# Two-layer retention and attention trunk: slice loads between weight blocks, a reordered first norm, and repeated identity products on TensorE

## The chip, the cores and the metric

The kernel runs on one core of one Trainium2 chip. The metric is the device time of one execution in microseconds. Before the change three runs gave 1913.54, 1915.96 and 1918.54 us, so the median is 1915.96 us.

## The reference, cut to what matters

Two layers (DEPTH = 2), d_model 1024, on 384 tokens in all: one prompt of 256 tokens and eight sample sequences of 16 tokens. All is float32.

```python
for l in range(DEPTH):
    mods = silu(c) @ w_ada[l] + b_ada[l]            # 1024 -> 6*1024, one row per sequence (9 rows)
    sh1, sc1, gt1, sh2, sc2, gt2 = split(mods, 6)
    h  = rmsnorm(x, g_mix) * (1 + sc1) + sh1
    u  = h @ w_in          # ret q,k,v,gate | att q,k,v | two merge gates
    y_r = gate * groupnorm(retention(rotary(q_r), rotary(k_r), v_r))      # 8 heads
    y_a = attention(rmsnorm(q_a), rmsnorm(k_a), v_a, rel_bias)            # 8 heads, own band / cache
    mixed = sigmoid(m_r) * (y_r @ w_br_ret) + sigmoid(m_a) * (y_a @ w_br_att)
    x  = x + gt1 * (mixed @ w_out)
    h2 = rmsnorm(x, g_ffn) * (1 + sc2) + sh2
    x  = x + gt2 * (relu(h2 @ w_up)**2 @ w_down)
```

The outputs are the final x of both groups, the retention states and the key and value rows.

## The kernel before, in words

**Split products.** Each float32 weight block and each activation is held as a high part (rounded to fp32r) and a low part (the rest). A product is three matmuls: high x high, low x high, high x low. SyncE (SP) loads weight blocks of 512 KB into a ring of four `raw` slots (`load`, L395 to L400; L395 waits until the block four places earlier has been split). ScalarE copies a block to `whi` (`high`, L679), VectorE subtracts to get `wlo` (`low`, L956); both have two slots. TensorE uses a block in `token_products` (L1407, 18 matmuls that stream 512 columns) or `products` (L1383, 24 matmuls that stream 384 columns).

**Order of the work.** It is written out by hand, one instruction stream for each engine, tied by semaphores. For each layer: the norm; the stage S_V (attention values, 8 blocks); 8 heads (8 blocks each, the attention and retention of the head before woven between the blocks); S_MERGE (2 turns of 20 blocks); S_OUT (`w_out`, 2 turns of 4 blocks); the second norm; S_UP (8 turns of 4 blocks); S_DOWN (4 turns of 8 blocks).

**The modulation.** `w_ada` is cut in slices of 512 columns, 2 MB each. A slice is multiplied by silu(c) on TensorE (`ada_product`, L1430), VectorE copies the result to `ada_s` (`ada_rows`, L1004), TensorE transposes it (`ada_turned`), VectorE adds the bias and writes `modT` (`ada_cols`, L1010). Layer 0's first four slices are loaded whole before the first norm needs them (two halves: slices 0 and 2, then 1 and 3). The last two slices of each layer go into `adaf_w`, which lies over memory that the merge still reads; so SP waits for `m_ready` (the last `mlo` of the merge) and issues the four 1 MB transfers (L467) in S_OUT, behind the fourth block of turn 0 and ahead of the first block of turn 1. Their products (`last_modulation`) come behind the second norm's sums.

**The first norm.** Squares of x are summed on ScalarE, POOL raises the mean to the power -1/2 (`x_rs`), VectorE puts it on a diagonal (`x_diag`), TensorE spreads it over the partitions with a ones matrix (L1517, into bank X[0]), VectorE copies it to `rstd` (L991). POOL writes the relative-position bias to DRAM (`band_d`), waits for that, and issues the copy to `skew_d` ahead of its part of the norm. TensorE waits for `rstd` before the first two slices of the modulation, since they use bank X[0]. When `modA` is there (L1020), VectorE splits blocks 0 and 1 and then makes the tiles k = 0 to 3 of the normed activation: `hp` (L1030) for the prompt; POOL makes `hs` (L542 multiply, L546 add) for the samples; ScalarE makes `hhi`; VectorE makes `hlo` (L1035, L1036) and so releases `h_ready`, for which the products wait.

**The head's start.** S_V uses six banks, the last two being X[1] and X[2]. ScalarE copies them out as `va_tok`. TensorE waits for the copies of banks 4 and 5 ahead of the first block of head 0, in both layers, though the head first uses X[0] and X[1] behind its sixth block.

Of the kernel before, what the change touches and what calls it, by code (L numbers as in the profile page):

```python
# [13 lines left out]
P = 128  # L14
# [134 lines left out]
def trunk(nc, x_prompt, x_sample, state_ret, cache_attn_k, cache_attn_v, c_prompt, c_sample, w_ada,  # L149
# [236 lines left out]
    def _(sp):  # L386
# [32 lines left out]
        for l in range(DEPTH):  # L419
# [38 lines left out]
            for i in range(S_OUT.turns):  # L458
                with cnt.turn(S_OUT.adds) as c:
                    for j in range(4):  # L460
                        load(c, j, [rows(w_out, l, j % 2, i * (2 * BC) + j // 2 * BC)])
                        if i == 0 and j == 3:
                            sp.wait_ge(m_ready, M0 + (l + 1) * KT)
                            for f in range(ADA_F):
                                at = (ADA0 + ADA_M + f) * ADA_C
                                for k in range(2):
                                    sp.dma_start(adaf_w[:, f, k * 4:k * 4 + 4, :],  # L467
                                                 w_ada[l, k * 4 * P:(k + 1) * 4 * P, at:at + ADA_C]
                                                 .rearrange("(k p) n -> p k n", p=P)).then_inc(adaf_full[f], 16)
            with sp.Fori(0, S_UP.turns) as i, cnt.turn(S_UP.adds) as c:  # L470
                for j in range(4):
                    load(c, j, [rows(w_up, l, j % 2, i * (2 * BC) + j // 2 * BC)])
# [20 lines left out]
    def _(pool):  # L493
# [30 lines left out]
        def first_tables(c):  # L524

            pool.wait_ge(band_ready, 1)
            dma(band_d, band[:, :]).then_inc(band_out, 16)
            pool.wait_ge(xms_ready, 1)
            g.tensor_tensor(x_rs[:, 0:NT], x_ms[:, 0:NT], mhalf[:, 0:NT], ALU.pow).then_inc(xrs_ready, 1)
            pool.wait_ge(band_out, 16)  # L530
            dma(skew_d, bass.AP(tensor=band_d.tensor, offset=CHUNK - 1, ap=[[BAND, DEPTH * HEADS], [-1, CHUNK], [1, SKEW]]))\
                .then_inc(skew_out, 16)
            pool.wait_ge(rstd_ready, 2)
            for k in range(KT):
                c.op(g.tensor_tensor(hs[:, k, :], xT[:, k, PR:TOK], rstd[:, PR:TOK], ALU.mult))
            for half in range(2):
                pool.wait_ge(moda_ready, half + 1)
                c.settle()
                for k in range(half * 4, half * 4 + 5):
                    d = seqs(hs[:, k % KT, :])  # L540
                    if k < half * 4 + 4:
                        c.op(g.tensor_tensor(d, d, modA[:, k, 1:NSEQ].unsqueeze(2).to_broadcast([P, SB, ST]), ALU.mult))  # L542
                    if k > half * 4:
                        pool.wait_ge(pool_own, c.now["own"] + (c.mine - 1 if k < half * 4 + 4 else c.mine))
                        d = seqs(hs[:, k - 1, :])
                        g.tensor_tensor(d, d, modT[:, k - 1, 1:NSEQ].unsqueeze(2).to_broadcast([P, SB, ST]),  # L546
                                        ALU.add).then_inc(hs_ready, 1)

        def norm_sample(c, shift):

# [392 lines left out]
    def _(dve):  # L943
# [44 lines left out]
                        x_rs[:, 0:NT].unsqueeze(2).to_broadcast([P, NT, P]), ALU.mult).then_inc(diag_ready, 1)  # L988
        dve.wait_ge(pre_a, 3)
        dve.wait_ge(spread_done, 1)  # L990
        v.tensor_copy(rstd[:, :], X[0][:, 0:TOK]).then_inc(rstd_ready, 2)  # L991

        def ada_rows(l, s, x):

# [44 lines left out]
        def norm(c, shift, gain, first=False):  # L1039

            if first:
                for half in range(2):
                    for n, s in enumerate(ADA_ORDER[2 * half:2 * half + 2]):
                        ada_rows(0, s, X[3 - 3 * n])
                        ada_cols(0, s, X[3 - 3 * n])
                    dve.wait_ge(mod_ready, 2 * half + 2)
                    modulated(c, shift, gain, half * 4, half * 4 + 4).then_inc(moda_ready, 1)
                    if half == 0:
                        low(c, 0)
                        low(c, 1)  # L1050
                    else:
                        low(c, 4)
                    dve.wait_ge(rstd_ready, 2)
                    dve.wait_ge(moda_ready, half + 1)
                    normed_tiles(c, shift, half * 4, half * 4 + 4)
                    if half == 0:
                        low(c, 2)
                        low(c, 3)
                return
            modulated(c, shift, gain, 0, KT).then_inc(moda_ready, 2)  # L1060
            low(c, 1)
            inverse_std(c)
            dve.wait_ge(rstd_ready, c.norm * 2 + 2)
            dve.wait_ge(moda_ready, c.norm * 2 + 2)
            if shift == 0:
                normed_tiles(c, shift, 0, 4)
                low(c, 2)
                low(c, 3)
                normed_tiles(c, shift, 4, KT)
            else:  # L1070
                normed_tiles(c, shift, 0, KT)
# [262 lines left out]
    def _(pe):  # L1334
# [181 lines left out]
        def mm(out, lhsT, rhs, start=True, stop=True):  # L1516
            return t.matmul(out, lhsT, rhs, start=start, stop=stop, skip_group_check=True)  # L1517

        def head(c, h, prev):

            H = c.head
            gr = S_HEAD.groups
# [18 lines left out]
                last_states(c)  # L1541
            gemm(5)

            pe.wait_ge(qk_norm, H + 1)
            pe.wait_ge(pair_ev, H * 4 + (P0 - 2))
            for n in range(NT):
# [60 lines left out]
        def last_modulation(l):  # L1607

            for f in range(ADA_F):
                pe.wait_ge(adaf_full[f], l * 32 + 32)  # L1610
                for k in range(KT):
                    ins = ada_product(X[1 + f], k, adaf_w[:, f, k, :], k == 0, k == KT - 1)
                ins.then_inc(ada_mm, 1)

        def up(c, l, first):
            for j in range(4):
# [16 lines left out]
                    ada_turned(l + 1, i, X[3])  # L1633


        pe.wait_ge(diag_ready, 1)
        for n in range(NT):
            ins = mm(X[0][:, n * P:(n + 1) * P], ones[:, :], x_diag[:, n, :])
        ins.then_inc(spread_done, 1)
        with cnt.turn({"norm": 1}, use=("norm",)) as c:  # L1640
            pass
# [1 line left out]
        def first_modulation(half):  # L1643

            if half == 0:
                pe.wait_ge(rstd_ready, 2)
            else:
                pe.wait_ge(mod_ready, 2)
            slices = ADA_ORDER[2 * half:2 * half + 2]
            for n, s in enumerate(slices):  # L1650
                for k in range(KT):
                    if k % 4 == 0:
                        pe.wait_ge(ada0_full[s][k // 4], 16)
                    ins = ada_product(X[3 - 3 * n], k, ada0_w[:, s, k, :], k == 0, k == KT - 1)
                ins.then_inc(ada_mm, 1)
            for n, s in enumerate(slices):
                ada_turned(0, s, X[3 - 3 * n])

        for l in range(DEPTH):
            if l:  # L1660
                with cnt.turn({"norm": 1}, use=("norm", "head")) as c:
                    norm(c)
            with cnt.turn(S_V.adds, also=("norm",)) as c:
                for j in range(8):
                    if l == 0 and j in (0, 3):
                        first_modulation(j // 3)
                    token_products(c, j, S_V.groups[j % 2], j // 2, normed=j % 2 == 0 and j < 6)
            with cnt.turn(S_HEAD.adds) as c:
                pe.wait_ge(acc_free[4], l + 1)
                pe.wait_ge(acc_free[5], l + 1)  # L1670
                head(c, 0, None)
            with pe.Fori(0, HEADS - 1) as h, cnt.turn(S_HEAD.adds) as c:
                head(c, h + 1, h)
            for i in range(S_MERGE.turns):
# [54 lines left out]
```

## Time and profile before

| what | value |
|---|---|
| median of 3 runs | 1915.96 us |
| the profiled execution's own time | 1917.57 us |
| its span | 1915.9 us |
| mean granted TensorE clock | 0.986 |
| TensorE busy | 1831.2 us, 96% |
| VectorE, ScalarE, POOL busy | 980.7, 735.0, 359.2 us |

The profiled execution's time is 1.67 us more than its span (start and end around the profiled work). Times in the rows are microseconds from the start of the span. A TensorE matmul's shown length overlaps the next; what counts is the distance from start to start. An engine's busy time doesn't count waits, and "idle before" names what ended a wait.

### The profile page before, as it was taken

The numbers are of one execution on the slowest core, as the hardware profiler recorded it, in microseconds if no ns is written. First come the engines' busy times: TensorE is split into PE (matmuls) and PEld (weight loads), VectorE is DVE, ScalarE is ACT, GpSimd is POOL, SyncE is SP. The second block draws the span as 40 slices with busy tenths as digits, with TensorE's granted clock in tenths as the row PEclk, the third lists the DMA queues.
The fourth block names the chain that finished last, engine by engine and source line by source line (L and its number), as shares of the span: only waits on it lengthen the run. The fifth ranks groups of instructions, "written<-read, shape, count | busy, mean of one in ns | idle before, by whom it ended". The sixth has DMA issues, their size and how long they took to land.

```text
span 1915.9 us, 34347 instructions
## 1 busy us (share of the span) xinstructions
PE 1831.2 (96%) x11834; PEld 1643.8 (86%) x11834; DVE 980.7 (51%) x1386; ACT 735.0 (38%) x1235; POOL 359.2 (19%) x443
## 2 busy tenths in 40 slices
PE   6999999999999999999989999999999999999998
PEld 5777777778999889999977777777789999899998
DVE  3455555556533475543354655555564335755333
ACT  3343444445332245432233444444453323444322
POOL 2143333333000030000022333333320001200000
PEclk8999999999999999999989999999999999999999
DMA  9676777774746624454537677777657465334342
GB/s 331 173 208 186 193 194 195 189 187 141 230 155 220 217 91 131 122 186 165 165 109 211 167 193 191 193 193 193 192 170 236 149 220 202 100 121 126 127 131 99
DMA packets 443675, 335.44 MB, mean 175 GB/s; under 512 B 150393, under 2 KB 402489, under 8 KB 443586
## 3 DMA queue, kind: packets, MB, share of 16 engines
q1 hardware_dynamic: 429152, 285.40, 50.8%
q0 software_dynamic: 12592, 44.99, 6.9%
q10 hardware_dynamic: 1842, 3.84, 0.5%
q8 instruction: 58, 0.95, 0.2%
q14 instruction: 31, 0.25, 0.0%
HBM read 307.40 MB, written 28.08 MB: 175 GB/s over the span
## 4 chain that ended last, share of the span: by engine, by line
PE 72%; issue 17%; DVE 5%; POOL 2%; DMA 2%; ACT 1%; SPq 0%; ACTq 0%; POOLq 0%; DVEq 0%
PE G L1383 47%; PE G L1407 13%; PE X L1517 7%; PE X L1343 2%; PE X L1430 2%; DVE wlo L956 2%; DMA raw<-in_w_out_dram 1%; DVE qk L1165 1%; POOL small L607 1%; DVE st L1126 1%; ACT prob L751 1%; POOL out_dram L509 0%; DMA out_dram<-st 0%; DMA crow<-in_c_sample_dram 0%; DVE hlo L1036 0%
## 5 line engine op out<-in xcount | busy, mean ns | idle before, releaser
L956 DVE TENSOR_TENSOR wlo<-raw,whi 128x1024 fp32r<-128x1024 f32 x369 | 478.3, 1297 | 656.9 <-ACT whi L679 656.1
L679 ACT ACTIVATE whi<-raw 128x1024 fp32r<-128x1024 f32 x369 | 391.2, 1060 | 814.9 <-PE G L1383 441.1
L1407 PE MATMUL G<-whi,hhi 128*128 128x512 f32 x832 | 342.9, 412 | 15.2 <-DVE hlo L1036 11.7
L1407 PE MATMUL G<-wlo,hhi 128*128 128x512 f32 x832 | 330.6, 397 | 0.0
L1407 PE MATMUL G<-whi,hlo 128*128 128x512 f32 x832 | 330.3, 397 | 0.0
L1383 PE MATMUL G<-hhi,whi 128*128 128x384 f32 x768 | 260.7, 339 | 5.8 <-DVE hlo L1036 5.8
L1383 PE MATMUL G<-hhi,wlo 128*128 128x384 f32 x768 | 257.6, 335 | 0.0
L1383 PE MATMUL G<-hlo,whi 128*128 128x384 f32 x768 | 257.4, 335 | 0.0
L1407 PEld LDWEIGHTS G<-whi,hhi 128*128 128x128 f32 x832 | 160.0, 192 | 64.6 <-issue 19.7
L1383 PE MATMUL G<-ysp,whi 128*128 128x384 f32 x768 | 198.0, 338 | 0.0
L1407 PEld LDWEIGHTS G<-wlo,hhi 128*128 128x128 f32 x832 | 159.7, 192 | 35.7
L1407 PEld LDWEIGHTS G<-whi,hlo 128*128 128x128 f32 x832 | 160.2, 193 | 30.2
L1383 PE MATMUL G<-fhi,whi 128*128 128x384 f32 x512 | 172.3, 337 | 0.0
L1383 PE MATMUL G<-fhi,wlo 128*128 128x384 f32 x512 | 171.2, 334 | 0.0
L1383 PE MATMUL G<-flo,whi 128*128 128x384 f32 x512 | 171.1, 334 | 0.0
L1383 PEld LDWEIGHTS G<-hhi,whi 128*128 128x128 f32 x768 | 144.6, 188 | 10.9 <-DVE hlo L1036 7.8
L1383 PEld LDWEIGHTS G<-hlo,whi 128*128 128x128 f32 x768 | 144.7, 188 | 0.0
L1383 PEld LDWEIGHTS G<-hhi,wlo 128*128 128x128 f32 x768 | 144.6, 188 | 0.0
L1383 PEld LDWEIGHTS G<-ysp,whi 128*128 128x128 f32 x768 | 137.2, 188 | 4.1 <-issue 3.8
L376 POOL TENSOR_TENSOR sq_sum<-sq 128x384 f32<-128x384 f32 x4 | 5.0, 1255 | 668.3 <-ACT sq L714 668.3
L1383 PE MATMUL G<-ysp,wlo 128*128 128x384 f32 x384 | 128.7, 335 | 0.0
L1383 PEld LDWEIGHTS G<-fhi,whi 128*128 128x128 f32 x512 | 96.1, 188 | 1.8 <-issue 1.6
(197 smaller groups left out, 2358.3 us busy)
## 6 DMA issues: line engine op xcount, KB each, us to landing
raw<-in_w_in_dram SPq DMA_DIRECT2D x256, 128.0 KB
raw<-in_w_in_dram SPq DMA_DIRECT2D x128, 256.0 KB
ada_w<-in_w_ada_dram SPq DMA_DIRECT2D x64, 512.0 KB, 4.9
raw<-in_w_up_dram SPq DMA_DIRECT2D x64, 512.0 KB
raw<-in_w_down_dram SPq DMA_DIRECT2D x64, 512.0 KB
raw<-in_w_in_dram SPq DMA_DIRECT2D x49, 512.0 KB
kc<-in_cache_attn_k_dram SPq DMA_DIRECT2D x64, 256.0 KB, 5.9
vc<-in_cache_attn_v_dram SPq DMA_DIRECT2D x32, 512.0 KB, 8.2
```

The lines of the kernel that those rows point to most:

```text
L376: ops.tensor_tensor(sq_sum[:, :], sq[:, 0, :], sq[:, 1, :], ALU.add).then_inc(sq_used, 2)
L607: g.tensor_tensor(qk_rs, qk_ms, mhalf[:, 0:6], ALU.pow).then_inc(qk_pow, 1)
L679: return a.activation(out, in_, ACT.Copy)
L751: a.activation(onorm[:, t, :], src, ACT.Square, accum_out=o_ss[:, t:t + 1]).then_inc(oss_ready, 1)
L956: v.tensor_tensor(wlo[:, j % SPLIT, :, :], raw[:, j % RAW, :, :], whi[:, j % SPLIT, :, :].bitcast(F32), ALU.subtract).then_inc(blk_split, 1)
L1126: v.scalar_tensor_tensor(out=s2, in0=s2, scalar=gS[:, 0:1], in1=X[q][:, :], op0=ALU.mult, op1=ALU.add).then_inc(pair_ev, 1)
L1165: c.op(v.tensor_tensor(q4, q4, qk_rs.rearrange("p (t a) -> p t a", a=2).unsqueeze(3).to_broadcast([P, NT, 2, DH]), ALU.mult))
L1343: return t.transpose(out, in_, ident[0:k, 0:k])
L1383: ins = t.matmul(G[b][:, 0:TOK], w[:, s, k, n * P:(n + 1) * P], x[:, k0 + k, :], start=first and k == 0 and x is hi and w is whi, stop=las ...
L1407: ins = t.matmul(B[b][:, :], x[:, kp * WK + k, n * P:(n + 1) * P], w[:, k, :], start=first and k == 0 and x is hhi and w is w_hi, stop=las ...
L1430: ins = t.matmul(x[32 * g:32 * g + 32, 0:P], cT[:, k, :], w[:, g * P:(g + 1) * P], start=start, stop=stop, skip_group_check=True)
L1517: return t.matmul(out, lhsT, rhs, start=start, stop=stop, skip_group_check=True)
```

## The change

- **S_OUT, both layers, SP:** in turn 1 each of the four block loads is followed by one of the four 1 MB transfers into `adaf_w`. The wait for `m_ready` stands before each of them, the first behind the load of turn 1's first block.
- **First norm, POOL:** the copy to `skew_d`, with its wait for `band_out`, goes behind the first half of the samples' tiles.
- **First norm, VectorE:** `low(c, 0)` goes between `ada_rows` and `ada_cols` of the first slice; `low(c, 1)` goes between tiles 0 to 1 and tiles 2 to 3.
- **First norm, TensorE:** the spread goes to bank G[2], so the modulation no longer waits for `rstd`. In each half the first slice's transposition goes into the middle of the second slice's products.
- **Identity products:** `steady(n)` issues n products of the ones matrix with the identity (128 columns) into X[2], which nobody reads: 6 before the wait for `x_diag`, 8 before the first half of the modulation, 10 behind it, 20 behind the norm at the start of layer 1. `last_modulation` issues 8 more into X[3] in each layer.
- **Head start, TensorE:** the waits for banks 4 and 5 go behind the sixth block of head 0, in both layers.

```diff
@@ SP, S_OUT
                     for j in range(4):
                         load(c, j, [rows(w_out, l, j % 2, i * (2 * BC) + j // 2 * BC)])
-                        if i == 0 and j == 3:
+                        if i:
                             sp.wait_ge(m_ready, M0 + (l + 1) * KT)
-                            for f in range(ADA_F):
-                                at = (ADA0 + ADA_M + f) * ADA_C
-                                for k in range(2):
-                                    sp.dma_start(adaf_w[:, f, k * 4:k * 4 + 4, :],
+                            f, k = j // 2, j % 2
+                            at = (ADA0 + ADA_M + f) * ADA_C
+                            sp.dma_start(adaf_w[:, f, k * 4:k * 4 + 4, :], w_ada[l, k * 4 * P:(k + 1) * 4 * P, at:at + ADA_C]
...
@@ POOL, first_tables
-            pool.wait_ge(band_out, 16)
-            dma(skew_d, ...).then_inc(skew_out, 16)
             pool.wait_ge(rstd_ready, 2)
...
+                if half == 0:
+                    pool.wait_ge(band_out, 16)
+                    dma(skew_d, ...).then_inc(skew_out, 16)
@@ VectorE
-        v.tensor_copy(rstd[:, :], X[0][:, 0:TOK]).then_inc(rstd_ready, 2)
+        v.tensor_copy(rstd[:, :], G[2][:, 0:TOK]).then_inc(rstd_ready, 2)
@@ VectorE, norm, first
                         ada_rows(0, s, X[3 - 3 * n])
+                        if n == half == 0:
+                            low(c, 0)
                         ada_cols(0, s, X[3 - 3 * n])
                     dve.wait_ge(mod_ready, 2 * half + 2)
                     modulated(c, shift, gain, half * 4, half * 4 + 4).then_inc(moda_ready, 1)
-                    if half == 0:
-                        low(c, 0)
-                        low(c, 1)
-                    else:
+                    if half:
                         low(c, 4)
                     dve.wait_ge(rstd_ready, 2)
                     dve.wait_ge(moda_ready, half + 1)
-                    normed_tiles(c, shift, half * 4, half * 4 + 4)
                     if half == 0:
+                        normed_tiles(c, shift, 0, 2)
+                        low(c, 1)
+                        normed_tiles(c, shift, 2, 4)
                         low(c, 2)
                         low(c, 3)
+                    else:
+                        normed_tiles(c, shift, 4, KT)
@@ TensorE, head (values is l + 1 for head 0, whose two waits ahead of it are gone)
             gemm(5)
+            if prev is None:
+                for b in (4, 5):
+                    pe.wait_ge(acc_free[b], values)
             pe.wait_ge(qk_norm, H + 1)
@@ TensorE, last_modulation
                 ins.then_inc(ada_mm, 1)
+            for _ in range(8):
+                mm(X[3][:, 0:P], ones[:, :], ident[:, :])
@@ TensorE
+        def steady(n):
+            for _ in range(n):
+                mm(X[2][:, 0:P], ones[:, :], ident[:, :])
+        steady(6)
         pe.wait_ge(diag_ready, 1)
         for n in range(NT):
-            ins = mm(X[0][:, n * P:(n + 1) * P], ones[:, :], x_diag[:, n, :])
+            ins = mm(G[2][:, n * P:(n + 1) * P], ones[:, :], x_diag[:, n, :])
@@ TensorE, first_modulation
             if half == 0:
-                pe.wait_ge(rstd_ready, 2)
+                steady(8)
...
+                    if n and k == 3:
+                        ada_turned(0, slices[0], X[3])
                 ins.then_inc(ada_mm, 1)
-            for n, s in enumerate(slices):
-                ada_turned(0, s, X[3 - 3 * n])
+            ada_turned(0, slices[1], X[0])
+            if half == 0:
+                steady(10)
@@ TensorE, start of layer 1
                     norm(c)
+                steady(20)
```

## Rows read from the trace of the kernel before

**Rows 1.** The page, part 1: busy time, share of the span, instructions.

```profile
PE 1831.2 (96%) x11834; PEld 1643.8 (86%) x11834; DVE 980.7 (51%) x1386; ACT 735.0 (38%) x1235; POOL 359.2 (19%) x443
```

**Rows 2.** PE's waits, whole run: total us, times, longest us.

```profile
PE X L1343 <- DVE st L1126: 34.0, 14, 2.4
...
PE G L1383 <- DVE hlo L1036: 5.8, 5, 2.5
```

**Rows 3.** Windows: length, busy of each engine, PEclk, DMA share, GB/s.

```profile
30.90:37.70 6.80, 5.21 (x12) 4.11 (x13) 4.08 (x11) 2.34 (x8) 2.34 (x5) 0.51 1.05 395
...
669.10:672.60 3.50, 3.50 (x13) 3.50 (x12) 2.12 (x4) 0.89 (x2) 1.74 (x1) 0.52 0.47 145
...
983.70:990.00 6.30, 6.29 (x15) 4.95 (x16) 3.58 (x7) 0.72 (x3) 4.20 (x9) 0.51 0.00 0
```

**Rows 4.** PE's order of time, S_OUT turn 1: start us, us, matmul, [idle before].

```profile
667.71 0.44 PE L1383 MATMUL G<-mhi,whi 128*128 128x384 f32 x1 [3.46 <-DVE wlo L956]
...
1612.82 0.44 PE L1383 MATMUL G<-mhi,whi 128*128 128x384 f32 x1 [2.16 <-DVE wlo L956]
```

**Rows 5.** SP's order of time in S_OUT of layer 0, the issues.

```profile
649.83 2.21 SPq L467 DMA_DIRECT2D adaf_w<-in_w_ada_dram  x4
652.30 9.63 SPq L400 DMA_DIRECT2D raw<-in_w_out_dram  x4
```

**Rows 6.** ScalarE's order of time, turn 1's first block.

```profile
665.34 1.06 ACT L679 ACTIVATE whi<-raw 128x1024 fp32r<-128x1024 f32 x1 [7.34 <-DMA raw<-in_w_out_dram]
```

**Rows 7.** Windows again: S_OUT while only these transfers run.

```profile
655.00:658.00 3.00, 3.00 (x19) 3.00 (x18) 2.09 (x5) 1.99 (x3) 0.00 (x0) 1.00 1.06 411
```

**Rows 8.** PE's order of time, layer 1's first product.

```profile
983.71 0.80 PE L1407 MATMUL G<-whi,hhi 128*128 128x512 f32 x1 [6.07 <-DVE hlo L1036]
```

**Rows 9.** PE's order of time: float32 products that stream 128 columns.

```profile
18.07 1.62 PE L1517 MATMUL X<-x_diag,ones 128*128 128x128 f32 x6 [2.21 <-DVE x_diag L987]
...
122.47 1.05 PE L1517 MATMUL X<-va_tok,pT 128*128 x8
```

**Rows 10.** PE's order of time, the opening.

```profile
20.44 5.38 PE L1430 MATMUL X<-ada_w,cT 128*32 128x128 f32 x128 [0.75 <-DVE rstd L991]
...
26.57 0.33 PE L1343 MATMUL X<-ident,ada_s 128*128 128x128 f32 x1 [0.49 <-DVE ada_s L1004]
32.49 0.80 PE L1407 MATMUL G<-whi,hhi 128*128 128x512 f32 x1 [5.59 <-DVE hlo L1036]
```

**Rows 11.** VectorE's order of time, from `modA` to the first `hp`.

```profile
27.17 0.20 DVE L1020 SCALAR_TENSOR_TENSOR modA<-modT,gT 128x36 f32<-128x36 f32 x1
27.29 2.57 DVE L956 TENSOR_TENSOR wlo<-raw,whi 128x1024 fp32r<-128x1024 f32 x2
29.78 1.71 DVE L1030 SCALAR_TENSOR_TENSOR hp<-xT,modA,rstd 128x256 f32<-128x256 f32 x3
```

**Rows 12.** POOL's order of time, the opening.

```profile
20.48 3.35 POOL L535 TENSOR_TENSOR hs<-xT,rstd 128x128 f32<-128x128 f32 x8 [1.24 <-DVE rstd L991]
27.53 2.59 POOL L542 TENSOR_TENSOR hs<-hs,modA 128x128 f32<-128x128 f32 x2 [3.69 <-DVE modA L1020]
...
30.62 0.58 POOL L542 TENSOR_TENSOR hs<-hs,modA 128x128 f32<-128x128 f32 x1
```

**Rows 13.** ScalarE's order of time, block 0 in the opening.

```profile
24.38 1.06 ACT L679 ACTIVATE whi<-raw 128x1024 fp32r<-128x1024 f32 x1 [8.32 <-DMA raw<-in_w_in_dram]
```

**Rows 14.** The DMA view of the first 80 us: count, KB, us to landing.

```profile
skew_d<-band_d POOLq DMA_DIRECT2D x1, 1280.0 KB, 12.8
```

**Rows 15.** PE's order of time, from S_V to head 0.

```profile
72.41 0.39 PE L1407 MATMUL X<-whi,hlo 128*128 128x512 f32 x1
72.64 0.39 PE L1407 MATMUL X<-wlo,hhi 128*128 128x512 f32 x1
74.00 0.47 PE L1407 MATMUL G<-whi,hhi 128*128 128x512 f32 x1 [0.98 <-ACT va_tok L679]
```

**Rows 16.** VectorE's order of time, head 0's block 1.

```profile
76.16 1.22 DVE L956 TENSOR_TENSOR wlo<-raw,whi 128x1024 fp32r<-128x1024 f32 x1 [4.37 <-ACT whi L679]
```

More of the change, by code:

```diff
@@ L461, in _ @@
                         load(c, j, [rows(w_out, l, j % 2, i * (2 * BC) + j // 2 * BC)])
-                        if i == 0 and j == 3:
+                        if i:
                             sp.wait_ge(m_ready, M0 + (l + 1) * KT)
-                            for f in range(ADA_F):
-                                at = (ADA0 + ADA_M + f) * ADA_C
-                                for k in range(2):
-                                    sp.dma_start(adaf_w[:, f, k * 4:k * 4 + 4, :],
-                                                 w_ada[l, k * 4 * P:(k + 1) * 4 * P, at:at + ADA_C]
-                                                 .rearrange("(k p) n -> p k n", p=P)).then_inc(adaf_full[f], 16)
+                            f, k = j // 2, j % 2
+                            at = (ADA0 + ADA_M + f) * ADA_C
+                            sp.dma_start(adaf_w[:, f, k * 4:k * 4 + 4, :], w_ada[l, k * 4 * P:(k + 1) * 4 * P, at:at + ADA_C]
+                                         .rearrange("(k p) n -> p k n", p=P)).then_inc(adaf_full[f], 16)
             with sp.Fori(0, S_UP.turns) as i, cnt.turn(S_UP.adds) as c:
@@ L529, in first_tables @@
             g.tensor_tensor(x_rs[:, 0:NT], x_ms[:, 0:NT], mhalf[:, 0:NT], ALU.pow).then_inc(xrs_ready, 1)
-            pool.wait_ge(band_out, 16)
-            dma(skew_d, bass.AP(tensor=band_d.tensor, offset=CHUNK - 1, ap=[[BAND, DEPTH * HEADS], [-1, CHUNK], [1, SKEW]]))\
-                .then_inc(skew_out, 16)
             pool.wait_ge(rstd_ready, 2)
@@ L547, in first_tables @@
                                         ALU.add).then_inc(hs_ready, 1)
+                if half == 0:
+                    pool.wait_ge(band_out, 16)
+                    dma(skew_d, bass.AP(tensor=band_d.tensor, offset=CHUNK - 1,
+                                        ap=[[BAND, DEPTH * HEADS], [-1, CHUNK], [1, SKEW]])).then_inc(skew_out, 16)
         def norm_sample(c, shift):
@@ L1517, in mm, with head @@
             return t.matmul(out, lhsT, rhs, start=start, stop=stop, skip_group_check=True)
-        def head(c, h, prev):
+        def head(c, h, prev, values=None):
             H = c.head
@@ L1668, in _ @@
             with cnt.turn(S_HEAD.adds) as c:
-                pe.wait_ge(acc_free[4], l + 1)
-                pe.wait_ge(acc_free[5], l + 1)
-                head(c, 0, None)
+                head(c, 0, None, l + 1)
             with pe.Fori(0, HEADS - 1) as h, cnt.turn(S_HEAD.adds) as c:
```

## The prediction, written before the changed kernel ran

> **What bounds the kernel now.** I read the page's busy times first. TensorE is busy 96% of the span, 1831.2 of 1915.9 us [rows 1], VectorE 51%; so a change counts only where it shortens a time in which TensorE stands still or runs at its lower clock. That leaves 85 us of standing still. PE's waits tell where: 34.0 us are 14 waits in the heads for the states' update, which the change doesn't touch, and the rest are single waits at the stages' edges [rows 2]. Then the windows around those edges: the granted clock is 0.51 (the 1.2 GHz level) from 30.9 to 37.7, 0.52 from 669.1 to 672.6 and 0.51 from 983.7 to 990.0, each time behind a wait of PE of several us, while PE is working again [rows 3]. Last, each engine's order of time around each edge, for what it waited on. All edits lie at such edges. A difference under 0.3% (5.7 us) couldn't be told from no change here.
>
> **S_OUT, both layers (the largest term).** The first block of turn 1 is late: PE stood 3.46 us in layer 0 and 2.16 us in layer 1 [rows 4]. SP issued the four 1 MB slices at 649.83 and the block only at 652.30, though its slot had been free since the split of turn 0's first block; SP stood at the wait for `m_ready` [rows 5]. The block came behind 4 MB, and ScalarE waited 7.34 us for it, until 665.34 [rows 6]. Afterwards the block is issued ahead of that wait, so it has nothing to stand behind. The next three each stand behind one slice. With these transfers alone the queue moved 411 GB/s [rows 7]: 1.5 MB are 3.8 us, and PE takes 24 matmuls x 0.17 us = 4.1 us for a block (0.17 is 384/512 of the 0.227 us between the starts of two 512-column matmuls [rows 15]). So 1.5 MB fit in a block, and each block is issued more than a block ahead. The last slice lands some 15 us before its products. Worth 3.46 + 2.16 = 5.6 us. Behind the stall in layer 0 PE was busy 3.50 us at 0.52 [rows 3]: 3.50 x 0.48 = 1.7 us, which go with the stall that preceded them. Sum 7.3 us. Bounds: 7.3, and 0 if the stall turns up at a later block; a loss would need a slice and a block to take over 4.1 us, and even all 4 MB in front of one block cost only the 3.46 us above.
>
> **Layer 1's first norm: 20 identity products.** PE stands 6.07 us until 983.71 [rows 8]. One product is like those that stream 128 columns: four of them (eight instructions) took 1.05 us at full clock, the last one's tail in it, so 0.22 each of issue; three took 1.62 us at the lower clock, 0.54 each [rows 9]. 20 x 0.22 = 4.4 us end before the 6.07 are over, even 20 x 0.26 = 5.2 do. They are queued ahead of the layer's first block, but that waits for VectorE's `hlo`, not for PE. If the clock is then full, the 6.29 us of work at 0.51 from 983.7 on [rows 3] lose 6.29 x 0.49 = 3.1 us. I take 3.0. Bounds: 3.1 and, with all 20 at the lower clock, 20 x 0.54 - 6.07 = 4.7 us lost. I take the upper, since PE comes to them from dense work at full clock.
>
> **`last_modulation`: 8 products.** 8 x 0.22 = 1.8 us in waits of about 2.5 us (the longest of the five in [rows 2]). What a full clock would give is small: PE there works at the pace of the norm's tiles; three of those five waits are short, 0.8 us in all (5.8 less twice 2.5), and they come between tiles at full clock. 0.2 us; bounds 1.7 (half of such a slow stretch as in S_OUT) and a loss of 2 x (8 x 0.54 - 2.5) = 3.6 us.
>
> **The opening.** Terms in order of time.
> - *Six and eight products, no wait for `rstd`.* Before `x_diag` PE stood 2.21 us [rows 9] and 0.75 us before the modulation [rows 10]. 6 x 0.22 = 1.3 fit the first gap; 8 x 0.22 = 1.8 start as soon as the spread is queued, so the modulation starts near 20.6 instead of 20.44. Its 128 instructions took 5.38 us, mostly at the lower clock. If the products raise it, they end at 24.3 instead of 25.8. Yet that gain isn't paid out, because of the next item.
> - *`low(c, 0)` between `ada_rows` and `ada_cols`.* It needs ScalarE's `whi`, whose block landed at 24.38 and was done at 25.44 [rows 13]. The subtraction takes 1.2 us, to 26.7. Then `ada_cols`, `ada_rows` of slice 2, PE's transposition, `ada_cols`, `modA`: 1.2 us (as from 26.12 to 27.37 now), 27.9 against 27.37 [rows 11]. The copy to `skew_d`, 12.8 us in flight from 18.4 [rows 14], is no longer in front of that block, which I put at 1 us sooner: `modA` at 26.9 to 27.9. I take no change for it. Bounds 0.5 either way. The wait holds the second slice's copy up, and behind that TensorE's transposition and POOL's tiles.
> - *Both subtractions leave the path.* They took 2.57 us between `modA` and the first `hp` [rows 11]. Now VectorE makes `hp` 0 and 1 at once, 0.57 each. POOL's two multiplies took 2.59 us beside the subtractions, 0.42 each alone and 0.58 beside `hp` [rows 12]. So: multiply, multiply, add = 1.75 us, ScalarE's copy 0.35, VectorE's two `hlo` 1.1, and 0.3 of hand-overs: first product 3.5 us behind `modA`, where it was 5.1 (32.49 [rows 10] less 27.37). Gain 1.6 us. Block 1's `wlo` is needed 4.1 us after the first product and done 2.4 us after it. Bounds 0.5 and 2.5.
> - *Ten products* fill part of the 5.59 us [rows 10] before the first block. They are 2.2 us at full and 5.4 us at the lower clock, in a gap of about 4; issued behind a transposition that itself waits for VectorE, they can still end late by 1 us. The blocks' stretch at 0.51, 5.21 us busy [rows 3], costs 2.55 us now. PE still stands idle for some 2 us ahead of the ten, so I take 1.5 of the 2.55. Bounds 2.6 and -1.
> - *The transposition inside the products* saves one of the transpositions behind the products, and the wait of 0.49 [rows 10] stays: 0.1 us in each half, counted as 0.2.
> - *G[2], the `skew_d` copy* cost nothing: POOL's issue lies behind its tiles, the head reads `skew_d` 30 us after it would land.
>
> Sum of the opening 3.3 us.
>
> By the Trainium skill, page "GPSIMD Engine Reference", section "8. Key points", GpSimd shares its SBUF interfaces with VectorE and contends with VectorE instructions that run in a 2-port mode or have two SBUF inputs. `hp` has two SBUF inputs too, so by that rule alone POOL would stay at the 1.29 us of the first two multiplies, and the gain of the two subtractions would be 1.6 - 1.4 = 0.2 us, the total 13.4. The rows show the clash with both, but 0.58 beside `hp` against 1.29 beside the subtractions; I go by them.
>
> **Head 0's start, both layers.** PE stood 0.98 us for the copy of the last bank [rows 15]. That goes. What is late next is block 1's `wlo`, ready at 77.38 [rows 16], held by ScalarE's copies and two DMA issues, which don't move. Block 0 would start at 72.87 (0.227 behind the last start [rows 15]) and end 18 x 0.227 = 4.1 us later, 76.96; PE then waits until 77.45. Before, block 1 started at 74.08 + 4.09 = 78.17. So 0.7 us, twice by the same pattern: 1.3 us (layer 1's is 0.1 shorter). Bounds 0 and 2.0.
>
> **Sum.** 7.3 + 3.0 + 0.2 + 3.3 + 1.3 = 15.1 us. From the profiled execution's own 1917.57 us (span 1915.9 and 1.67 around it) that gives 1902.5; from the median 1915.96, 1.6 lower, 1900.9. I say 1902.
>
> **Rivals.**
> - *The identity products don't hold the clock* (60 short products count too little beside dense blocks). For it: the three short products at 18.07, behind 24 short transpositions, ran at the lower clock [rows 9]. Against: there they stood between waits, and the four in the head, between blocks, ran at the full one. The 3.0, the 1.5 and the 0.2 are gone: 10.4 us stay, 1905.5 on the median. 15%.
> - *The first block of the opening waits on a landing.* `low(c, 0)` now stands in front of the modulation on VectorE. If block 0 lands 2 us later, `modA` is 2.5 us later, and the opening gives 1 instead of 3.3: 1903.5. 10%.
> - *The stall of S_OUT moves instead of going*: a slice in front of each block holds the second or third, half of 7.3 is left. 1904.5 to 1908. 6%.
> - *What the edges gain the heads take back.* The 14 waits of 2.4 us in the heads [rows 2] sit close to what makes the clock fall; shifted in time, three more of them might be followed by a slow stretch of 1.7 us: 5 us back, 1906; it can as well be three fewer, 1896. 5% beyond my range.
> - *Slower: the identity products run at the lower clock and come out longer than their gaps.* 24 in the opening, 20 at layer 1, 16 in `last_modulation`, at 0.54 us: 13.0, 10.8 and 8.6 us in gaps of some 8, 6.07 and 5: 5 + 4.7 + 3.6 = 13.3 us in front of the products that wait for nothing else. The rest of the change gives 7.3 less the kept 1.7, 1.6, 1.3 = 8.5. Net 4.8 us slower, 1920.7. It decides from 0.30 us a product on (6.07/20). 4%.
>
> **How the numbers follow.** The forecast has 60%. Its own range is 1897 to 1907: the terms' bounds and one or two slow stretches of the heads on either side. The rivals at 1903.5 to 1908 stretch it to 1896 to 1909. Faster than 1910.2 takes in the forecast and all rivals but the last and a part of S_OUT's and the heads': 0.90. Within 0.3% 0.06, slower 0.04.
>
> **What would show each step.** S_OUT: no wait of PE for `wlo` in turn 1, SP's issues alternating, the first block's `whi` without a DMA wait, granted clock 1.0 there. Layer 1: the window behind the norm at 1.0, 20 ones-by-identity products that end before the first `hlo`. Opening: POOL's first two multiplies near 1.2 us together, first product near 30.8, the stretch at the lower clock shorter. `last_modulation`: the waits for `hlo` unchanged in their end. Head 0: no wait for `va_tok`, one of 0.4 us for `wlo`. I'm wrong if a wait of PE for `wlo` or `whi` comes up in S_OUT's later blocks, if `modA` comes later than 28.5, or if the products end behind the `hlo` that they precede.

## The result, and the profile after

| | before | after |
|---|---|---|
| median | 1917.11 us (4 runs, 1913.54 to 1918.54) | 1899.4 us (4 runs, 1898.58 to 1899.89) |
| profiled execution, its span | 1917.57, 1915.9 us | 1898.58, 1896.9 us |
| mean granted TensorE clock | 0.986 | 0.995 |

The ratio is 0.9914, 95% interval 0.9901 to 0.9927: faster, as forecast (1902, range 1896 to 1909). The two profiled spans differ by 19.0 us. Seven marks on TensorE split it:

| mark, start in us | before | after | ahead by | gained since the mark above |
|---|---|---|---|---|
| first product of layer 0 | 32.49 | 30.66 | 1.83 | 1.83 |
| second half's last transposition | 51.78 | 47.72 | 4.06 | 2.23 |
| head 0's first transpositions, layer 0 | 100.01 | 95.30 | 4.71 | 0.65 |
| second norm's sum, layer 0 | 686.03 | 674.35 | 11.68 | 6.97 |
| first product of layer 1 | 983.71 | 972.10 | 11.61 | -0.07 |
| head 0's first transpositions, layer 1 | 1046.52 | 1031.42 | 15.10 | 3.49 |
| second norm's sum, layer 1 | 1629.61 | 1610.57 | 19.04 | 3.94 |

Nothing is gained behind the last mark (1915.9 - 1896.9 = 19.0).

**Busy time.** The page, part 1, of the changed kernel. TensorE's busy time is 2.3 us more than in [rows 1], though the run is 19 us shorter: 120 instructions are new, and they stand where it stood idle.

```profile
PE 1833.5 (97%) x11954; PEld 1648.6 (87%) x11954; DVE 980.5 (52%) x1386; ACT 734.8 (39%) x1235; POOL 357.4 (19%) x443
```

**TensorE's waits**, changed kernel, in the columns of [rows 2]. The head's waits are as they were. The long waits for `hlo` at the norms' ends have turned into identity products and a rest: in `products` 8 waits of 2.6 us in all (five of 5.8 before), in `token_products` one of 1.6. The waits for `ada_s` and `wlo` grew to 2.6 and 2.1; both are met below.

```profile
PE X L1345 <- DVE st L1128: 34.0, 14, 2.4
...
PE G L1385 <- DVE hlo L1035: 2.6, 8, 0.6
PE X L1345 <- DVE ada_s L1003: 2.6, 2, 2.2
...
PE G L1409 <- DVE wlo L955: 2.1, 4, 0.7
PE G L1409 <- DVE hlo L1035: 1.6, 1, 1.6
```

**S_OUT, layer 0.** SP's order of time, the answer to [rows 5]: block, slice, block, slice. The first block of turn 1 was issued long before (it is the fifth of the x5). TensorE has no wait there in either layer, so [rows 4] have no answering row.

```profile
620.15 19.64 SPq L400 DMA_DIRECT2D raw<-in_w_out_dram  x5
643.47 0.37 SPq L466 DMA_DIRECT2D adaf_w<-in_w_ada_dram  x1
645.15 0.39 SPq L400 DMA_DIRECT2D raw<-in_w_out_dram  x1
645.58 1.00 SPq L466 DMA_DIRECT2D adaf_w<-in_w_ada_dram  x1
647.73 0.39 SPq L400 DMA_DIRECT2D raw<-in_w_out_dram  x1
```

The windows over the same transfers (columns of [rows 3]): the queue still moves up to 399 GB/s, TensorE is busy all the time, and the clock is full where [rows 3] had 0.52.

```profile
655.00:659.00 4.00, 4.00 (x25) 4.00 (x24) 2.98 (x7) 1.09 (x2) 0.00 (x0) 1.00 1.06 399
...
659.00:663.00 4.00, 4.00 (x25) 4.00 (x24) 1.59 (x2) 1.83 (x3) 2.77 (x2) 1.00 0.81 277
```

**The opening**, TensorE's order of time in the changed kernel, the answer to [rows 10]. The modulation's products now take 2.83 + 1.08 us where they took 5.38, with one transposition between. Then TensorE stands 2.15 us for the second slice's copy. The ten products (20 instructions) take 4.02 us: mostly at the lower clock in this profile. The first block isn't held by them: the `hlo` that it needs is done at 30.60 and it starts at 30.66.

```profile
16.20 1.61 PE L1519 MATMUL X<-ident,ones 128*128 128x128 f32 x12 [0.48 <-DVE bT L981]
17.84 0.94 PE L1519 MATMUL G<-x_diag,ones 128*128 128x128 f32 x6
18.61 1.95 PE L1519 MATMUL X<-ident,ones 128*128 128x128 f32 x16
20.50 2.83 PE L1432 MATMUL X<-ada_w,cT 128*32 128x128 f32 x96
...
23.51 1.08 PE L1432 MATMUL X<-ada_w,cT 128*32 128x128 f32 x32
26.75 0.33 PE L1345 MATMUL X<-ident,ada_s 128*128 128x128 f32 x1 [2.15 <-DVE ada_s L1003]
26.91 4.02 PE L1519 MATMUL X<-ident,ones 128*128 128x128 f32 x20
30.66 0.56 PE L1409 MATMUL G<-whi,hhi 128*128 128x512 f32 x1
```

VectorE's order of time, the `hlo` that releases the first block:

```profile
29.98 0.62 DVE L1035 SCALAR_TENSOR_TENSOR hlo<-hp,modT,hhi 128x256 fp32r<-128x256 f32 x1
```

The windows of the same kernel: 0.51 while the ten run, 1.00 for the blocks where [rows 3] had 0.51. (In the changed kernel's repetition, experiment 3, no stretch of the opening is at the lower clock, and the ten take 2.40 us.)

```profile
27.40:30.90 3.50, 3.50 (x19) 3.48 (x18) 2.74 (x6) 1.53 (x4) 3.20 (x8) 0.51 1.05 401
30.90:37.70 6.80, 6.80 (x32) 5.58 (x32) 5.10 (x10) 2.37 (x5) 1.19 (x2) 1.00 1.05 396
```

VectorE's order of time, then POOL's, both of the changed kernel, for [rows 11 and 12]: one subtraction ahead of `modA`, `hp` right behind it, and POOL's first two multiplies in 0.95 us where they took 2.59.

```profile
25.16 1.23 DVE L955 TENSOR_TENSOR wlo<-raw,whi 128x1024 fp32r<-128x1024 f32 x1 [2.35 <-ACT whi L678]
...
27.34 0.20 DVE L1019 SCALAR_TENSOR_TENSOR modA<-modT,gT 128x36 f32<-128x36 f32 x1
27.66 1.27 DVE L1029 SCALAR_TENSOR_TENSOR hp<-xT,modA,rstd 128x256 f32<-128x256 f32 x2
```

```profile
27.70 0.95 POOL L537 TENSOR_TENSOR hs<-hs,modA 128x128 f32<-128x128 f32 x2 [4.79 <-DVE modA L1019]
```

**Layer 1's norm and head 0**, TensorE's order of time, for [rows 8 and 15]: 40 instructions in 4.63 us, 1.61 us of waiting left of 6.07; and at head 0's block 1 a wait of 0.33 us in place of the 0.98 ahead of block 0.

```profile
73.34 0.50 PE L1409 MATMUL G<-whi,hhi 128*128 128x512 f32 x1 [0.33 <-DVE wlo L955]
...
965.86 4.63 PE L1519 MATMUL X<-ident,ones 128*128 128x128 f32 x40
972.10 0.51 PE L1409 MATMUL G<-whi,hhi 128*128 128x512 f32 x1 [1.61 <-DVE hlo L1035]
```

### The profile page after: what moved, and what is told of

Read it like the earlier page. It is cut to its first block, busy times and chain, and to the rows that moved or that the text cites. A ratio compares the mean times of both kernels' runs of the same rounds, so it can differ in the third digit from the quotient of the medians.

```text
span 1896.9 us, 34585 instructions
## 1 busy us (share of the span) xinstructions
PE 1833.5 (97%) x11954; PEld 1648.6 (87%) x11954; DVE 980.5 (52%) x1386; ACT 734.8 (39%) x1235; POOL 357.4 (19%) x443
## 4 chain that ended last, share of the span: by engine, by line
PE 74%; issue 16%; DVE 5%; POOL 2%; ACT 1%; DMA 1%; SPq 0%; POOLq 0%; DVEq 0%; ACTq 0%
PE G L1385 49%; PE G L1409 14%; PE X L1519 7%; PE X L1345 2%; PE X L1432 2%; DVE wlo L955 1%; DVE qk L1167 1%; POOL small L606 1%; DVE st L1128 1%; DMA raw<-in_w_in_dram 1%; ACT prob L750 1%; POOL out_dram L507 0%; DVE hlo L1035 0%; DVE hlo L1034 0%; DVE rstd L1015 0%
```

## The experiments

Ten kernels ran, in three jobs; in each the kernel before ran beside them (medians 1915.25, 1914.83 and 1914.89 us).

**1. S_OUT's edit alone**, on the kernel before.

```diff
-                        if i == 0 and j == 3:
+                        if i:
                             sp.wait_ge(m_ready, M0 + (l + 1) * KT)
...
+                            f, k = j // 2, j % 2
+                            sp.dma_start(adaf_w[:, f, k * 4:k * 4 + 4, :], ...)   # one 1 MB slice for each block
```

> The kernel before with only the S_OUT edit on SP (each of turn 1's block loads followed by one 1 MB slice). Theory, that the stall at turn 1's first block and the slow stretch behind it are the change's largest single term: no wait of TensorE for wlo in S_OUT turn 1 in either layer, granted clock full there, 5.6 + 1.7 = 7.3 us less, so 1909 to 1911. Rival, that the stall moves to a later block: a wait for wlo of 1 to 3 us at block 2 or 3, 1912 to 1915. Rival, that the edit's gain came from elsewhere in the changed kernel: no difference, 1916.

Measured: 1906.49 us (1906.18 to 1907.61), ratio 0.995 (0.9937 to 0.9964). That is 8.8 us below the median beside it, 7.3 forecast. No wait of TensorE is left in turn 1 and no lower clock behind it; the window over the transfers:

```profile
652.00:660.00 8.00, 8.00 (x48) 8.00 (x48) 4.72 (x8) 2.63 (x5) 1.29 (x1) 1.00 1.05 381
```

The stall didn't move to a later block. The lower clock behind it was the stall's price. The 1.5 us above the forecast lie elsewhere. In this kernel's profile TensorE's marks are 5.3 us ahead in layer 0's part, with three slow stretches (TensorE working at the lower granted clock) in its heads as before, and 4.0 us in layer 1's, with two where the kernel before had three. So the edit itself gives 5.3 and about 2.3; one slow stretch fewer (1.7) and a shorter one at layer 1's norm (0.6) are how the runs fell (experiment 3).

**2. The changed kernel without any identity product.** The four `steady` calls and the loop of eight are taken out.

```diff
-            for _ in range(8):
-                mm(X[3][:, 0:P], ones[:, :], ident[:, :])
...
-        steady(6)
-                steady(8)
-                steady(10)
-                steady(20)
```

> The changed kernel without any of the 60 identity products. Theory, that they hold TensorE's clock at the opening (2.5 us) and at layer 1's norm (3.0 us) and do nothing in last_modulation: slow stretches come back behind both waits, 5.5 us slower than the changed kernel's 1899.4, so 1905. Rival, that the first products only gain from starting sooner and the clock would have been full anyway: 1900. Rival, that the identity products are also behind the two slow stretches fewer in the heads (4 for 6): 1908 to 1909.

Measured: 1904.62 us (1902.09 to 1905.89), ratio 0.9936 (0.9922 to 0.9949), 5.1 above the changed kernel run beside it (1899.56). The total fits the theory, its parts less so. The first product came at 30.50, no later than with them (30.42 in the changed kernel's repetition), so they gain nothing by an earlier start; the blocks behind it ran slow and the second half's last transposition came 2.55 us later (49.97 against 47.42). Layer 1 lost 1.4 us, not 3.0 (from its first product to head 0's transpositions 60.78 against 59.34). And 2.0 us of this profile have another cause, which I hadn't thought of. TensorE's and ScalarE's order of time in this kernel:

```profile
30.50 0.80 PE L1409 MATMUL G<-whi,hhi 128*128 128x512 f32 x1 [3.58 <-DVE hlo L1035]
...
77.64 0.50 PE L1409 MATMUL G<-whi,hhi 128*128 128x512 f32 x1 [2.33 <-DVE wlo L955]
```

```profile
72.41 2.50 ACTq L908 DMA_DIRECT2D out_dram<-va_tok  x1
75.27 2.00 ACT L678 ACTIVATE whi<-raw 128x1024 fp32r<-128x1024 f32 x2 [3.41 <-issue]
```

ScalarE's second DMA issue of the attention values took 2.50 us, where it took 0.49 in the kernel before and in the changed one, and held the `whi` of head 0's block 1. The last rival, that the identity products are also behind the heads' fewer slow stretches, isn't borne out: this profile has five, between the changed kernel's four and the kernel before's six.

**3. Eight identity products in each head too**, and the changed kernel once more beside it.

```diff
+            pe.wait_ge(acc_free[2], c.now["bank2"] + S_HEAD.uses[2])
+            for _ in range(8):
+                mm(G[2][:, 0:P], ones[:, :], ident[:, :])
             pe.wait_ge(qk_norm, H + 1)
             pe.wait_ge(pair_ev, H * 4 + (P0 - 2))
```

> The changed kernel, with 8 more identity products in each head, into bank G[2], ahead of the wait of 2.4 us for the states' update. Theory, that the slow stretches in the heads come from that wait and that such products fill it: no slow stretch in the heads (4 in the changed kernel's profile, 1.7 us each), 6.8 us faster than 1899.4, so 1892 to 1894; the wait itself stays and ends at the same time. Rival, that what paces the heads is VectorE and the slow stretches only fill its slack: 1899. Rival, that 8 products (1.8 to 2.1 us) run over in the waits of 1.26 us of the two first heads and hold up what follows: 1 to 2 us slower than the theory.

> The changed kernel once more, beside the others: 1898 to 1900, and 3 to 6 slow stretches in the heads if their number is a matter of how each run falls; exactly 4 if the kernel's own timing fixes it.

Measured: 1891.63 us (1890.82 to 1891.74) with them, ratio to before 0.987 (0.9855 to 0.9886); 1899.56 us (1898.36 to 1901.51) without, ratio 0.9913 (0.99 to 0.9927). The 14 waits are 9.0 us where they were 34.1, with the products in the rest, and the heads' windows show it; first the waits and the window of layer 0's heads in the kernel with eight, then the window in the changed kernel's repetition:

```profile
PE X L1345 <- DVE st L1128: 9.0, 14, 0.6
```

```profile
100.00:540.00 440.00, 435.50 (x2888) 366.93 (x2887) 251.75 (x363) 184.08 (x361) 129.30 (x143) 1.00 0.69 193
```

```profile
100.00:540.00 440.00, 422.95 (x2749) 352.16 (x2748) 250.50 (x362) 183.01 (x360) 129.15 (x143) 0.99 0.68 191
```

7.9 us faster than the repetition, more than the 6.8 of four stretches, since the repetition's profile has six: the slow stretches in the heads are real time, and a filled wait has none. That refutes the rival of VectorE's pace. The rival of the run-over came true without a cost: in layer 0's head 0 the wait was only 1.26 us and the transpositions behind the eight start 0.40 us later (95.43 for 95.03), but the next block starts at 96.65 where it started at 96.62 in the repetition, since it waits for its `wlo` either way. How many slow stretches there are changes from run to run: the granted clock fell six times in the heads in the kernel before's profile, four times in the changed kernel's, six times in its repetition's, and four to six times in all eight profiles without products in the heads. So 3.4 of the 19.0 us between the two profiles (two stretches of 1.7) are how the runs fell. The mean clock of each run tells the same: of 29 runs of the kernel before, the six at 0.989 took 1913.4 to 1914.1 us, the six at 0.985 or 0.986 took 1916.4 to 1919.0. With the heads' waits filled the four runs spread over 0.9 us, the repetition's five over 3.2.

**4. The two subtractions back behind `modA`**, in the changed kernel.

```diff
-                        if n == half == 0:
-                            low(c, 0)
...
+                    if half == 0:
+                        low(c, 0)
+                        low(c, 1)
...
-                        normed_tiles(c, shift, 0, 2)
-                        low(c, 1)
-                        normed_tiles(c, shift, 2, 4)
+                        normed_tiles(c, shift, 0, 4)
```

> The changed kernel with the subtractions of blocks 0 and 1 back between modA and the first hp. Theory, that they and their clash with POOL's multiplies were on the path: modA 0.8 us or so earlier than the changed kernel's 27.54 (nothing waits for block 0's landing any more), POOL's first two multiplies 2.5 us again where they took 0.95, first product 5.1 us behind modA where it was 3.1: at 31.7 to 32, that is 1.1 to 1.5 us later than 30.4 to 30.7, total 1900 to 1901. Rival, that POOL would clash as much with the hp multiplies (two inputs from SBUF) and only VectorE's own 2.5 us count: POOL's pair unchanged near 1 us, first product 2.5 us behind hp. Rival, that the first product waits for a landing anyway: no change.

Measured: 1902.19 us (1901.82 to 1903.69), ratio 0.9929 (0.9912 to 0.9945): 2.6 us above the changed kernel's repetition, which ran in another job (the fastest run of this one took 1901.82 us, the slowest repetition 1901.51), and more than the 1.1 to 1.5 expected. `modA` was done at 25.75, 1.8 us before the changed kernel's 27.54 where 0.8 was expected; and the first product came 5.84 us behind it, not 5.1, since VectorE also waited 0.74 us for block 1's `whi`. TensorE's order of time and the window behind it:

```profile
24.95 0.33 PE L1344 MATMUL X<-ident,ada_s 128*128 128x128 f32 x1 [0.41 <-DVE ada_s L1003]
25.12 2.40 PE L1518 MATMUL X<-ident,ones 128*128 128x128 f32 x20
31.59 0.80 PE L1408 MATMUL G<-whi,hhi 128*128 128x512 f32 x1 [4.08 <-DVE hlo L1035]
```

```profile
30.90:37.70 6.80, 6.11 (x15) 4.84 (x16) 2.83 (x9) 1.24 (x4) 1.16 (x2) 0.54 1.04 395
```

The first product is 1.2 us later, as expected, by those two misses. But the ten products end at 27.5, TensorE stands 4.08 us, and the blocks run at 0.54 again, as with no products at all. By head 0's transpositions it is 3.77 us behind the repetition (98.80 against 95.03): 1.17 of the start and 2.6 of the clock. (The profile's total is only 2.2 us above the repetition's: it has five slow stretches in the heads, not six.) With all the products in place the lower clock came back when the subtractions did, and experiment 2 shows it back without the products: the blocks' clock needs both. No run takes the ten products out alone, so their share beside the fourteen before them isn't shown. POOL's pair took 1.61 us and its next multiply, beside the second subtraction, 1.38; beside `hp` alone it is 0.95 for the pair:

```profile
25.91 1.61 POOL L537 TENSOR_TENSOR hs<-hs,modA 128x128 f32<-128x128 f32 x2 [3.05 <-DVE modA L1019]
...
27.83 1.38 POOL L537 TENSOR_TENSOR hs<-hs,modA 128x128 f32<-128x128 f32 x1
```

The rival, that POOL would clash as much with `hp`, is refuted.

**5. The head's start alone**, on the kernel before.

```diff
-                pe.wait_ge(acc_free[4], l + 1)
-                pe.wait_ge(acc_free[5], l + 1)
-                head(c, 0, None)
+                head(c, 0, None, l + 1)      # the two waits behind gemm(5)
```

> The kernel before with only the waits for banks 4 and 5 moved behind head 0's sixth block. Theory: the wait of 0.98 us for the last copy goes in both layers and one of 0.3 to 0.4 us for block 1's wlo comes, 0.6 to 0.7 us less each; from the end of S_V's last matmul to head 0's transpositions 0.65 us shorter. In the total 1.3 us, hard to tell: 1914 to 1916. Rival: ScalarE's DMA issues (one took 2.5 instead of 0.5 us in the kernel without identity products) hold block 1, and nothing is gained.

Measured: 1917.45 us (10 runs, 1912.9 to 1918.44), ratio 1.0008 (0.9998 to 1.0017), the median beside it 1914.83: no gain in the total. In the profile layer 1 has the expected 0.30 us wait at block 1 in place of 0.98. Layer 0 has 1.56 us, behind a DMA issue of ScalarE that took 1.72, so it is 0.6 us slower there: the rival's case. Nine profiles of all these kernels have the moved waits and ScalarE's issues in their old place; in two of them the issue was long, in the other seven layer 0's wait for block 1 is 0.33 to 0.35. On the total it is inconclusive: the 1.3 us expected lie under the slow stretches' spread. What shows the gain is the wait in the profiles.

**6. No eight products behind `last_modulation`**, otherwise the changed kernel.

```diff
-            for _ in range(8):
-                mm(X[3][:, 0:P], ones[:, :], ident[:, :])
```

> The changed kernel without the 8 identity products behind each last_modulation. Theory, that TensorE goes at the pace of VectorE's tiles there, so a slow stretch costs next to nothing: wait 2.5 us instead of 0.56, the next stage's 24 matmuls in the same time to 0.2 us, total 1899 to 1900, with or without a slow stretch there. Rival, that a slow stretch there costs half of its 3.4 us, once or twice: 1901 to 1903.

Measured: 1900.33 us (1899.48 to 1900.95), ratio 0.9918 (0.9902 to 0.9935), 0.8 above the repetition. In this profile a slow stretch did fall on S_UP's start, in both layers (granted 0.78 in the window from 683 to 687, 0.73 from 1622 to 1626). From the first matmul of layer 0's S_UP to the first transposition, 48 matmuls on, 10.55 us passed, 10.16 in the changed kernel; in layer 1 10.52 and 10.17. It cost 0.4 us each time, not 1.7: TensorE goes at the pace of VectorE's tiles there (VectorE is busy 4.00 of 4.00 us in both windows). The kernel before had such a stretch in layer 0 too, from 696.4 to 699.8, and took 10.21 us: there it cost next to nothing.

**7. The eight in the heads, and block 0's subtraction one step later.**

```diff
-                        if n == half == 0:
+                        if n and half == 0:
                             low(c, 0)
```

> The changed kernel with 8 identity products in each head's wait and block 0's subtraction one step later, between ada_rows and ada_cols of the second slice. Theory, that in the changed kernel the second slice's copy and transposition wait for block 0's landing, 1.6 to 2.2 us of TensorE standing, and that the subtraction fits beside TensorE's transposition: modA 0.5 to 0.9 us earlier, first product at 29.7 instead of 30.4; total 1890.9 against 1891.6 with the 8 products alone. Rival, that the block's whi at 25.1 is late for either place: no difference.

Measured: 1891.04 us (1890.59 to 1891.27), ratio 0.987 (0.9854 to 0.9887). TensorE's order of time: the second transposition waits 0.41 us where it waited 1.21 to 2.15 in the profiles with the subtraction one step earlier, and the first product comes 0.54 us sooner than in kernel 3 (30.41).

```profile
25.34 0.33 PE L1345 MATMUL X<-ident,ada_s 128*128 128x128 f32 x1 [0.41 <-DVE ada_s L1003]
...
29.87 0.50 PE L1409 MATMUL G<-whi,hhi 128*128 128x512 f32 x1 [1.97 <-DVE hlo L1035]
```

So in the changed kernel `low(c, 0)` did hold the modulation up for block 0's landing.

**8. ScalarE's two DMA issues later**, on kernel 7.

```diff
             high(c, 1)
+            if prev is None:
+                values_out()          # the two dma_start of va_tok, ahead of the stage before
             high(c, 2)
```

> The kernel with 8 identity products in each head and block 0's subtraction one step later (1891.0), and ScalarE's two DMA issues of the attention values behind head 0's second whi instead of ahead of it. Theory, that these issues (0.5 us each, one of them 1.7 and 2.5 us in two profiles) hold block 1: TensorE's wait of 0.30 to 0.35 us for block 1's wlo goes in both layers, 0.6 us less, 1890.4. Rival, that ScalarE's last copy of the banks is what holds the block: the wait stays above 0.2 us.

Measured: 1890.91 us (1889.48 to 1891.15), ratio 0.9871 (0.9854 to 0.9887). Both waits for block 1 are gone, `wlo` is waited for twice, 0.8 us in all, instead of four times. In the total 0.1 us, which these runs can't tell from nothing. In the profile more is gained than the 0.6 expected: 0.66 us in layer 0 and 0.62 in layer 1, each up to head 0's first transpositions. But it is one profile, of the fastest run (1889.48 us, mean clock 1.0); the other three took 1890.7 to 1891.2 with a mean clock of 0.998 or 0.999, that is, with some time at the lower clock, and why isn't known.

**9. Kernel 7 without the 20 products at layer 1's norm.**

```diff
-                steady(20)
```

> The kernel of 1891.0 us without the 20 identity products at layer 1's norm. Theory: a slow stretch comes back there and reaches into the first block; how far depends on how it falls, 0.8 us were lost in one profile, 2.5 in another and 3.0 in the kernel before: 1892 to 1894. Rival, that the products in the heads and elsewhere keep the clock and the 20 aren't needed: 1891.

Measured: 1893.62 us (1893.42 to 1894.06), ratio 0.9885 (0.9868 to 0.9901), 2.6 above kernel 7. TensorE's order of time and the window behind it:

```profile
968.09 0.79 PE L1409 MATMUL G<-whi,hhi 128*128 128x512 f32 x1 [6.07 <-DVE hlo L1035]
```

```profile
968.00:972.00 4.00, 3.91 (x9) 3.13 (x10) 3.66 (x8) 0.80 (x3) 4.00 (x9) 0.50 0.00 0
```

The rest of the kernel ran at the full clock, and still this stretch fell to the lower level: the 20 are needed, and the rival is refuted.

## Why the prediction was right, and where its sizes were off

- **S_OUT: right in mechanism and size.** 7.3 forecast. The marks give 6.97 in layer 0's part with one head stretch (1.7) in it, so 5.3, and 3.94 less 1.7 = 2.2 in layer 1's: 7.5. Alone 8.8 on the medians, and 5.3 and about 2.3 on its profile's marks. The rival of the moving stall is refuted.
- **Layer 1's 20 products: right.** 3.0 forecast; 3.49 less the head's start 0.65 is 2.8; 2.6 when only they are taken out. The row used for one product (0.22) held: 40 instructions in 4.63 us. The kernel without any lost only 1.4 there, since the slow stretch ended sooner behind the first product.
- **The opening: right in mechanism, each size somewhat off.** 3.3 forecast, 4.06 measured. The step "both subtractions leave the path" was put at 1.6 and gave 2.0: the first product came 3.12 us behind `modA`, not 5.12. `modA` at 27.54 was 0.17 late, inside 26.9 to 27.9, so the start gained 1.83. The landing I expected 1 us sooner isn't to be seen: `whi` started at 24.07 for 24.38, but at 23.79 and 24.06 in the two other kernels that leave the `skew_d` copy in its old place, so no run shows that the copy's move gave anything. Neither it nor the spread's move to G[2] was run alone. What the products saved on the modulation went into the wait of 2.15 us, as forecast. The clock gave 2.2, where I took 1.5. The ten products ran at the lower clock themselves, 4.02 us for 20 instructions, and that cost nothing: "they can still end late" didn't happen. In the repetition they took 2.40 us, and there too the first product came 3.12 us behind `modA`; it came 0.24 us earlier because block 0's `whi` did. The transposition inside the products gave nothing (-0.06 in the second half; forecast 0.2).
- **`last_modulation`: nothing in these two profiles** (-0.07), though the kernel before had a slow stretch there in layer 0; 0.4 a layer in experiment 6; 0.2 forecast. At 0 to 0.8 us for both layers it is too small for the medians.
- **The head's start: 0.65 in layer 0**, as in the working, but not steadily: ScalarE's DMA issue can take it back.
- **The heads: not in my sum, 3.4 us between the two profiles.** I had it as a rival in both directions. Six stretches in the repetition say that it is how the runs fell and not the change. So a part of the 19.0 us is luck: on the medians the gain is 17.7 us in the change's own measurement and 15.7 in the job with the repetition (1915.25 less 1899.56), against 15.1 in my sum.
- **Two slips in the working**, neither in the forecast's sum. 15.1 less 1.4 is 13.7, not 13.4, for the total by the rule on POOL and VectorE. And the rival of the late landing, 2.3 us off the sum, gives 1903.2 on the median, not 1903.5.
- **POOL beside VectorE.** In this case's traces the clash of POOL's multiplies with VectorE's two-input `hp` is weak (0.95 us for two, where one takes 0.42 with VectorE idle) and the clash with the subtractions strong (1.29 and 1.38 us each). The working by rows was the right one. The Trainium skill, page "GPSIMD Engine Reference", section "8. Key points", names VectorE instructions with two SBUF inputs as a source of contention, without a size; the traces agree that both kinds slow POOL, and differ by more than a factor of two between them.

## What to carry to other kernels

Where TensorE is the bound, look behind each of its waits for the granted clock: the stall of 3.46 us in S_OUT cost another 1.7 here, the one of 2.16 us in layer 1 nothing more, and the heads' 14 waits of up to 2.4 us cost 1.7 us in four to six cases a run. A wait that can't be removed can be made cheap by products that nobody reads, provided that they are shorter than the wait and leave little of it behind them: with 1.35 to 2.40 us left ahead of the first block the clock stayed full here, with 4.08 us left it didn't. Big transfers that aren't urgent belong between urgent ones, behind a block that is already due. Before a step that waits for a landing is moved ahead in an engine's stream, see what stands behind it: the place one step later was 0.5 us better.

## What the runs showed of the hardware that I had not expected

- With identity products in the waits of the heads the mean granted clock is 0.997 to 1.0, and the four runs of a kernel lie within 0.6 to 1.7 us; without them the 29 runs of the kernel before spread over 5.5 us (1913.4 to 1919.0), and the mean clock in the records falls as the time rises.
- A DMA issue on ScalarE's queue took 2.50 and 1.72 us in two profiles and 0.49 or 0.50 us in the others, for the same 512 KB transfer at the same place (layer 0's start of head 0). What made it long isn't shown: the DMA share around the long ones was 1.16 and 1.14, and around a short one, in the kernel of experiment 3, 1.15 (70 to 74 us).
